# Head norms of the third block: a split square and two fp32r products with ones in place of one fp32 product

## The reference, cut to what matters

```python
def rmsnorm(x, g):
    xf = x.astype(jnp.float32)
    y = xf * lax.rsqrt(jnp.mean(xf * xf, axis=-1, keepdims=True) + EPS)
    return (y * g.astype(jnp.float32)).astype(x.dtype)

def mixer_c(n, w_in, gq, gk, w_out):
    q, k, v = _split(n @ w_in, (C_WIDTH, C_WIDTH, C_WIDTH))       # 3 x 1024 columns
    q = rmsnorm(q.reshape(bsz, s_len, N_HEADS_C, HEAD_DIM), gq)   # 8 heads of 128
    k = rmsnorm(k.reshape(bsz, s_len, N_HEADS_C, HEAD_DIM), gk)
    v = v.reshape(bsz, s_len, N_HEADS_C, HEAD_DIM)
    return stick_breaking(q, k, v).reshape(bsz, s_len, C_WIDTH) @ w_out
```

## Time and profile before

| | |
|---|---|
| time, median of 3 runs | 2190.1 us (2186.49 to 2190.47) |
| profiled execution, its own time | 2185.17 us |
| its span | 2183.4 us |
| TensorE busy | 2109.0 us, 97% of the span |
| GpSimd busy | 1407.2 us, 64% |
| VectorE busy | 923.9 us, 42% |
| ScalarE busy | 575.9 us, 26% |
| mean granted clock of TensorE | 0.993 of full speed |
| block C, from its first unit to its last norm | about 1576 to 1750 us of the span |

### The profile page before, as it was taken

The page is one execution under the profiler, slowest core; times in us unless marked ns, Lnnn a source line. Parts: engine busy times, 40 slices in busy tenths (PEclk is TensorE's granted clock), DMA queues, the critical chain, the costliest instruction groups (busy, mean ns, idle before and its releaser), DMA issues.

```text
span 2183.4 us, 32781 instructions
## 1 busy us (share of the span) xinstructions
PE 2109.0 (97%) x13144; PEld 1707.9 (78%) x13144; DVE 923.9 (42%) x1481; ACT 575.9 (26%) x1202; POOL 1407.2 (64%) x1642
## 2 busy tenths in 40 slices
PE   8999888999999999999999999999999989999999
PEld 6777777778888888766767888888877778888887
DVE  7887554624320122468987421121245554210210
ACT  3134424223320121214335220021145552200200
POOL 8875412844877777754551887777755528877874
PEclk9999999999999999999999999999999999999999
DMA  5222101322333333222211333333322103333332
GB/s 190 81 78 66 54 23 42 126 62 90 110 97 97 97 96 97 87 68 59 68 59 32 95 96 97 96 97 98 95 77 68 58 30 110 98 98 99 96 98 96
DMA packets 52754, 184.32 MB, mean 84 GB/s; under 512 B 7824, under 2 KB 7952, under 8 KB 52496
## 3 DMA queue, kind: packets, MB, share of 16 engines
q1 hardware_dynamic: 52336, 181.43, 26.9%
q10 hardware_dynamic: 288, 1.11, 0.2%
HBM read 180.42 MB, written 2.10 MB: 84 GB/s over the span
## 4 chain that ended last, share of the span: by engine, by line
PE 88%; DVE 8%; issue 1%; ACT 1%; DMA 1%; POOL 1%; SPq 0%; ACTq 0%; DVEq 0%; POOLq 0%
PE PB L1711 23%; PE PB L1712 23%; PE PB L1714 23%; PE PB L1697 11%; DVE AR L1000 3%; PE PB L1862 2%; PE PB L1784 2%; PE PB L1700 2%; DVE AR L1003 1%; ACT AR L530 1%; PE PB L1748 1%; DVE SM L1497 1%; DVE AR L1500 1%; PE PB L1751 1%; PE PB L1749 1%
## 5 line engine op out<-in xcount | busy, mean ns | idle before, releaser
L521 POOL TENSOR_TENSOR WL<-W,WH 128x256 fp32r<-128x256 f32 x1304 | 1044.5, 832 | 27.2
L1712 PE MATMUL PB<-AR_r,WL 128*128 128x512 f32 x2352 | 917.6, 390 | 0.0
L517 POOL TENSOR_SCALAR WH<-W 128x1024 fp32r<-128x1024 f32 x326 | 358.1, 1099 | 726.9 <-DMA W<-weights_in 726.6
L1714 PE MATMUL PB<-AR_r,WH 128*128 128x512 f32 x2352 | 581.0, 390 | 0.0
L1712 PEld LDWEIGHTS PB<-AR_r,WL 128*128 128x128 f32 x2352 | 442.6, 188 | 94.3 <-issue 4.5
L1714 PEld LDWEIGHTS PB<-AR_r,WH 128*128 128x128 f32 x2352 | 441.7, 188 | 91.4
L1711 PE MATMUL PB<-HN_r,WH 128*128 128x512 f32 x1184 | 473.9, 400 | 5.0 <-DVE AR L1000 3.4
L1711 PE MATMUL PB<-AR_r,WH 128*128 128x512 f32 x1168 | 456.6, 391 | 0.2 <-POOL WL L521 0.2
L530 ACT ACTIVATE AR<-AR 128x512 f32<-128x512 f32 (+4 forms) x268 | 156.1, 621 | 763.6 <-DVE AR L1003 668.6
L1003 DVE SCALAR_TENSOR_TENSOR AR<-PB,AR 128x512 f32<-128x512 f32 (+3 forms) x157 | 101.5, 648 | 442.8 <-PE PB L1714 392.9
L1000 DVE TENSOR_TENSOR H<-H,PB 128x512 f32<-128x512 f32 x80 | 55.0, 688 | 524.8 <-PE PB L1714 509.0
(11 more groups left out here) (124 smaller groups left out, 1322.2 us busy)
## 6 DMA issues: line engine op xcount, KB each, us to landing
W<-weights_in SPq DMA_DIRECT2D x326, 512.0 KB, 3.6
H<-x_in SPq DMA_DIRECT2D x8, 512.0 KB, 6.3
h_out<-H SPq DMA_DIRECT2D x8, 256.0 KB, 4.6
C<-constants_in SPq DMA_DIRECT2D x3, 512.0 KB, 4.6
H<-mem_in ACTq DMA_DIRECT2D x1, 1024.0 KB, 7.2
C<-constants_in SPq DMA_DIRECT2D x1, 800.0 KB, 12.2
V<-vectors_in SPq DMA_DIRECT2D x1, 640.0 KB, 10.8
C<-constants_in SPq DMA_DIRECT2D x1, 544.0 KB, 4.6
```

Source lines behind the costliest of these rows:

```text
L517: pool.tensor_scalar(WH[:, u % RING, :], w, 1.0, 1.0, ALU.mult, ALU.mult).then_inc(sems["w_round"], 1)
L521: low = pool.tensor_tensor(WL[:, u % RING, part], w[:, part], WH[:, u % RING, part].bitcast(F32), ALU.subtract)
L1712: pe.matmul(out, ll, rh, start=False, stop=False)
L1714: ins = pe.matmul(out, lhs(k)[0], rhs(k)[0], start=False, stop=stop and k == KT - 1)
```

## The change

For each of the 16 norms ScalarE writes the square twice: once rounded to fp32r (`CSH`), once in fp32 (`CSQ`). GpSimd subtracts the two into a rest `CSLOW` in fp32r. TensorE sums both with ones in fp32r (`ONES_R`, made once per run by a ScalarE copy of 128x128) into the same bank. The subtraction stands in GpSimd's stream of weight units: at the unit four places after head h's K unit, behind that unit's two waits and ahead of its rounding. TensorE's norm waits for `c_low` (GpSimd) where it waited for `c_sq` (ScalarE). Two semaphores, `v_in` and `mem_in`, become one, `act_in`, with the second wait at 32.

```diff
+        CSH, CSLOW, ONES_R = arr(46, 48), arr(61, 63), arr(63, 64)[:, 0, 0:P]
+        LOW_AT = {AT["c_in"] + c_unit(h, 1) + RING: h for h in range(8)}
...
                 pool.wait_ge(slot_loaded[u % RING], loads(u))
                 if u >= RING:
                     pool.wait_ge(sems["w_used"], u - RING + 1)
+                if u in LOW_AT:
+                    for c in range(2):
+                        pool.wait_ge(sems["c_sq"], 2 * LOW_AT[u] + c + 1)
+                        pool.tensor_tensor(CSLOW[:, c, :], CSQ[:, c, :], CSH[:, c, :].bitcast(F32), ALU.subtract).then_inc(sems["c_low"], 1)
                 w = W[:, u % RING, :]
...
-            act.dma_start(V[:, 0:FIRST_VECS], v_d[:, 0:FIRST_VECS]).then_inc(sems["v_in"], 16)
+            act.dma_start(V[:, 0:FIRST_VECS], v_d[:, 0:FIRST_VECS]).then_inc(sems["act_in"], 16)
...
-            act.dma_start(MT, mem_d).then_inc(sems["mem_in"], 16)
-            act.wait_ge(sems["mem_in"], 16)
+            act.dma_start(MT, mem_d).then_inc(sems["act_in"], 16)
+            act.wait_ge(sems["act_in"], 32)
...
             act.preload_act_table_set(LN_EXP)
+            f(ONES_R, cst("ones"), ACT.Copy).then_inc(*A.inc())
...
                         act.wait_ge(sems["c_ev"], 2 * hd + c + 1)
                         if hd:
                             act.wait_ge(sems["c_nm"], 2 * hd + c - 1)
+                        f(CSH[:, c, :], x[:, hd, :], ACT.Square).then_inc(*A.inc())
                         f(CSQ[:, c, :], x[:, hd, :], ACT.Square).then_inc(*A.inc("c_sq"))
...
             def c_norm(c, hd):
 
-                pe.wait_ge(sems["c_sq"], 2 * hd + c + 1)
+                pe.wait_ge(sems["c_low"], 2 * hd + c + 1)
                 take(7)
-                mm(PB[7][:, :], cst("ones"), CSQ[:, c, :]).then_inc(*T.inc("c_nm"))
+                mm(PB[7][:, :], ONES_R, CSLOW[:, c, :], stop=False)
+                mm(PB[7][:, :], ONES_R, CSH[:, c, :], start=False).then_inc(*T.inc("c_nm"))
                 free[7] = ("c_rln", 2 * hd + c + 1)
```

More of the change, by code:

```diff
@@ L231, in build @@
         names = ["w_used", "w_round", "w_split", "x_hi", "x_lo", "vt_ev", "vt_tr", "hid_sq", "hid_hi", "half_h", "act_step",
-                 "dve_step", "mem_in", "c_in", "c_rest", "v_in", "stored", "norm_h", "norm_sq", "norm_acc", "norm_ms",
+                 "dve_step", "act_in", "c_in", "c_rest", "stored", "norm_h", "norm_sq", "norm_acc", "norm_ms",
                  "norm_rs", "norm_out", "sq_used", "fin_sq", "fin_used", "fin_rs1", "fin_ms2", "fin_rs2", "rs_ab", "rs_tok", "rs_tok_ev",
@@ L242, in build @@
                  "og_act", "gla_out", "g_ede", "ke_in", "ke_tr", "ke_ev", "kv2_mm", "sh_ev", "go_mm", "go_sq", "go_nm", "go_ln", "go_rs",
-                 "go_ev", "c_sq", "c_nm", "c_rs", "c_sc", "c_rln", "c_abs", "c_exp", "c_l", "c_nl", "c_la", "c_prob"]
+                 "go_ev", "c_sq", "c_low", "c_nm", "c_rs", "c_sc", "c_rln", "c_abs", "c_exp", "c_l", "c_nl", "c_la", "c_prob"]
         sems = {n: ctx.enter_context(nc.semaphore(n)) for n in names}
@@ L552, in used @@
                 act.wait_ge(sems["w_used"], AT[name] + i + 1)
-            act.dma_start(V[:, 0:FIRST_VECS], v_d[:, 0:FIRST_VECS]).then_inc(sems["v_in"], 16)
+            act.dma_start(V[:, 0:FIRST_VECS], v_d[:, 0:FIRST_VECS]).then_inc(sems["act_in"], 16)
             act.preload_act_table_set(LN_EXP)
             act.wait_ge(sems["c_in"], 16)
-            act.wait_ge(sems["v_in"], 16)
+            act.wait_ge(sems["act_in"], 16)
             def square_mix(n):
@@ L1068, in _ @@
             dve.memset(PX[:, :, 0:1], 0.0).then_inc(*D.inc())
-            dve.wait_ge(sems["v_in"], 16)
+            dve.wait_ge(sems["act_in"], 16)
             dve.wait_ge(sems["c_in"], 16)
```

## The result

The changed kernel takes 2219.24 us (median of 5 runs, 2216.7 to 2225.01) against 2190.1 us (5 runs too): ratio 1.0143, 95% interval 1.0127 to 1.0158, so 29.1 us slower. The forecast was 2212 in a range of 2200 to 2225. The profiled execution took 2219.24 us, its span is 2217.4 us.

A forecast was written before the change was run, and what follows sets the result against it. The prediction took TensorE, busy for 97% of the span, as the bound. Waits of 17.3 us, net of the product gain, plus 4.7 us of clock loss made 22.0 us: 2190.1 + 22.0 = 2212.1 us, range 2200 to 2225.

The forecast's parts named there:

- The place of the wait: GpSimd at unit K+4 in block C: subtractions start only when that unit's weights have landed, and TensorE waits for them.
- The size of the waits: TensorE ahead of the norms of all eight heads: 17.3 us in all, the 6.4 us product gain already in it.
- The products: TensorE's 16 norms: two fp32r matmuls, 0.46 us, replace 0.86 us; 0.40 us back per norm, 6.4 us in all.
- covered cost: ScalarE's second squares push copies ahead of a transpose from head 3 on; costed at nothing, up to 3.2 us without cover.
- TensorE's clock: Granted clock falls to 0.50 behind the long waits of heads 0, 1 and 2: 3 x 1.57 = 4.7 us; upper bound 12.6.
- more than I count: Rival: subtractions of 1.77 us each and clock falls at heads 4 and 3 too; 2218.9 us, chance 0.22.
- main case: Waits for GpSimd in block C with the clock loss at three heads; 2207 to 2217 us, chance 0.50.
- faster: Rival: GpSimd subtracts before TensorE arrives, only the shorter products count; 2183.7 us, or 2186.9 with pushed ScalarE copies; chance 0.05.

The follow-up runs named there:

- ahead: Changed kernel with GpSimd's two subtractions ahead of the wait for the landed weights of unit K+4, not behind it; 2203.38 us, ratio 1.0056.
- no_rest: Changed kernel without GpSimd's subtraction; TensorE waits for the squares alone and sums the rounded squares twice in two fp32r products; 2190.83 us, ratio 1.0010.
- fill: Changed kernel with fp32 products of constants on TensorE ahead of each wait for the rest of Q, later overwritten; 2207.5 us, ratio 1.0078.
- fp32_wait: Changed kernel with its subtraction and waits, but TensorE sums the fp32 squares in one fp32 product, as before; 2226.41 us, ratio 1.0160.
- pool_round: Changed kernel, but heads 0 and 1 as before; for heads 2 to 7 GpSimd rounds and subtracts at units Q+4 and K+4, ScalarE squares once; 2189.6 us.
- mid_heads: As pool_round, but head 7 too keeps the fp32 product, so only heads 2 to 6 are changed; 2187.38 us, ratio 0.9981.
- act_squares: Kernel before with ScalarE's second square alone, written and not used; 2195.44 us, ratio 1.0026.

## Why the prediction was right, and where it was not

**The place of the wait: right, and shown.** GpSimd's pair follows the landed transfer in all eight heads, and TensorE waits for it ahead of all eight Q norms. `ahead` moved only this order and took 21.1 us out of the length up to the last K norm (17.7 out of that to the norm behind); `no_rest` took the subtraction away and with it all of the loss up to the last K norm.

**The size of the waits: near, in part by errors that offset each other.** 17.3 us forecast, 18.4 in `fill`, where the clock plays no part; to the end of the last K norm, as the forecast counts, it is 18.0. Head by head (start of the K norm against before, taken from `fill`) 4.5, 4.0, 2.9, 2.2, 2.0, 0.9, 1.0, 1.1 us, forecast to the end of it 4.0, 4.4, 3.0, 1.4, 2.0, 0.7, 0.9, 0.9. Three things are off. In heads 2 to 7 the forecast took the end of the norm before from the end of its record (1.02 us behind its start) and the end of the new one from the distance of matmuls (0.46 us behind it), which made each of six heads 0.16 us too short; put right, its own rows give 18.2. The subtraction is shorter than my 1.40 us; with about 1.25 us the measurement is nearer to the 1.28 us that follows from the Trainium skill (GPSIMD Engine Reference, Performance versus the Vector engine) than to twice the 256-column row. Against that, the K norms of heads 0 and 1 waited last not for GpSimd, as I had put it, but 0.87 us for ScalarE's Ln, which must empty bank 7 of the Q norm first; this is worth about 0.2 us a head in `fill`.

**The products: right.** 0.40 us per norm forecast; 0.38 in `fp32_wait`. In `pool_round`, where nothing is in their way, 73.20 us from the K norm of head 4 to that of head 7 against 75.52 before: 0.77 a head, 0.39 a norm.

**ScalarE: right as a covered cost.** I costed it at nothing, with up to 3.2 us if the cover were gone. Taken alone it cost 3.3 us up to the last K norm, heads 0 and 1 included, and 5.0 us to the norm behind the block.

**TensorE's clock: the mis-sized term.** The prediction said "So I add 3 x 1.57 = 4.7 us, and nothing for heads 3 to 7". It measured 13.3 us, the difference between the changed kernel and `fill`, more than the 12.6 us that the prediction gave as the bound for falls at all eight heads. Four things were wrong in it. The price of one fall was too low: counted at the start of the next Q norm, the four falls cost 4.5, 3.3, 2.6 and 2.9 us, not 1.57. The clock stayed low longer than behind the wait at 72 us: at head 0 until about 1606.5, while TensorE did the Q norm, waited 0.87 us more, and did the K norm, small products and the first part of the next unit. It fell in a fourth place, head 4, behind a wait of 2.00 us. And I took 2.45 us without a fall as safe, where the length of one wait does not settle it: in `no_rest` the clock was low behind 2.18 us at head 1 and not at head 0, in the changed kernel it was not low behind 2.27 us at head 3. The running count by head, changed kernel less `fill` at the start of each K norm: 0.5 us at head 0, 5.0 at head 1, 10.6 at head 2, 10.3 at head 3, 13.1 at head 4, 13.3 at heads 5 to 7. It holds for these two executions: in `fp32_wait`, with nearly the same waits, the clock fell at other heads and for shorter.

**The rest of the 34.0 us of span.** 31.7 us up to the last K norm, 2.6 us ahead of the block, where the code is the same but for the merged semaphore; where these come from is open. The median is 7 us above the 2212 of the forecast. In the profiles the block is 9.5 us longer than the forecast's 22.0 (31.5 us to the norm behind): 8.6 of these are the clock term and 0.8 the waits. With the 2.6 us ahead it would be 12; the profiled execution of before was 4.9 us below its median.

**The rival "more than I count", and luck.** The forecast's main case had 2207 to 2217 us of its own, and 2219.2 lies just above it, next to the 2218.9 of this rival. But not for its reasons: it had a subtraction of 1.77 us (measured 1.25) and falls of the clock at heads 4 and 3 (only head 4 fell). That the sum lands so near is luck; the mechanism is that of the main case, with a larger clock term.

**The rival "faster".** It named as its condition a subtraction that starts 1.5 to 3.8 us earlier in heads 2 to 7, and ahead of K's eviction in heads 0 and 1. With an earlier one in heads 2 to 7, and heads 0 and 1 left as before (`pool_round`), the block gained 4.0 us up to the last K norm, and the last rounds gave it back. The version that keeps heads 0, 1 and 7 as they were, `mid_heads`, is the fastest here, 0.19% below before.

## What to carry to other kernels

Before work is put into an engine with much free time, read what its stream waits for just ahead of that place: an instruction behind a wait for a transfer inherits the transfer's latency, and whoever waits for it does too. Where TensorE is the bound, a new wait can have two prices, the wait and what follows at half the clock; here the second was 13.3 us beside 18.4, and which waits brought it could not be told from their lengths. And a gain in the steady rounds has to be followed to the end of the block: in the last rounds another engine's chain may bound, and it may be the one that the new work slows down.

## What was not expected of the hardware

In this kernel the clock's fall behind a wait did not go by the wait's length alone: 1.61 us (`act_squares`, round 13), 2.00 us (head 4, changed kernel) and 2.18 us (`no_rest`, head 1) had it at 0.50 behind them, and 1.61 us (before, round 13), 1.99 us (`fp32_wait`, head 4), 2.18 us (`no_rest`, head 0), 2.27 us (head 3, changed kernel) and 2.45 us had not. Keeping TensorE at work with products whose result is thrown away held it at 1.00, and paid: 11.7 us of 2219 in the median. A VectorE instruction on 128x128 took 1.02 us while GpSimd rounded a unit (`pool_round`), 0.49 us while it split one (`mid_heads`, 1748.34), and 0.29 us while it was idle (`mid_heads`, 1750.87). Why the block begins up to 7 us later in some executions these runs leave open.
